# A bidirectional gated-delta scan: decay exponentials written into the decayed queries' tile, their loads issued earlier, and the last pair's norm work reordered

## What is computed

```python
def chunked_gated_delta(q, k, v, beta, log_alpha, s0):
    """S_t = a_t (I - b_t k_t k_t^T) S_{t-1} + b_t k_t v_t^T, o_t = S_t^T q_t"""
    g = jnp.cumsum(blk(log_alpha), axis=-1)
    a_mat = eye + einsum(kb, k) * dec_strict
    u_val = triangular_solve(a_mat, vb); w_key = triangular_solve(a_mat, kb * exp(g))
    qk = einsum(q, k) * dec_incl
    q_dec = q * jnp.exp(g)[..., None]
    k_end = k * jnp.exp(g_last - g)[..., None]
    def step(s, inp):
        v_new = u_c - w_c @ s
        o_c = qd_c @ s + qk_c @ v_new
        s = s * dl_c + ke_c^T @ v_new
        return s, o_c

def mixer(...):
    o_f, s_f = chunked_gated_delta(q, k, v, ...)          # forward
    o_b, s_b = chunked_gated_delta(rev(q), rev(k), ...)   # backward
    o = rmsnorm(o_f + rev(o_b), o_norm_w) * silu(gate)
    y = concatenate([y_conv, o]) @ w_out
```

## Time and profile before

| | us |
|---|---|
| median of 3 runs | 1591.64 |
| lowest, highest | 1590.41, 1592.5 |
| the profiled execution | 1592.61 |
| its span (first to last instruction) | 1590.7 |
| PE busy within it | 1524.4 (96%) |
| DVE, ACT, POOL busy | 936.8, 484.4, 403.1 |

### The profile page before, as it was taken

How to read it: one execution, slowest core, us unless ns; L and a number is a source line. 1 busy time by engine, 2 the same in 40 slices (tenths; PEclk the granted TensorE clock), 3 DMA queues, 4 the chain that set the end, 5 groups by cost and what they waited for, 6 DMA issues and landing times.

```text
span 1590.7 us, 24063 instructions
## 1 busy us (share of the span) xinstructions
PE 1524.4 (96%) x9744; PEld 1471.3 (92%) x9744; DVE 936.8 (59%) x1398; ACT 484.4 (30%) x904; POOL 403.1 (25%) x204
## 2 busy tenths in 40 slices
PE   5899999999989997999999999999999999999997
PEld 1798999999989887998999999999999999999996
DVE  2751463669987884337885276528643673467257
ACT  4332253221257675125311132121212210221024
POOL 0011111650233452130231123113222321223120
PEclk9999999999999998999999999999999999999999
DMA  9545124541434467120111111111111111111103
GB/s 360 217 158 184 68 82 127 158 128 70 141 114 127 142 205 268 40 67 1 40 54 41 41 40 43 51 41 40 40 40 41 47 47 40 41 40 40 40 1 119
DMA packets 74112, 142.60 MB, mean 90 GB/s; under 512 B 19212, under 2 KB 44372, under 8 KB 72340
## 3 DMA queue, kind: packets, MB, share of 16 engines
q1 hardware_dynamic: 70116, 131.38, 24.4%
q10 hardware_dynamic: 3456, 7.87, 1.3%
q0 software_dynamic: 432, 1.77, 0.3%
HBM read 120.34 MB, written 20.65 MB: 89 GB/s over the span
## 4 chain that ended last, share of the span: by engine, by line
PE 85%; DVE 7%; ACT 2%; issue 2%; DMA 2%; POOL 1%; DVEq 0%; ACTq 0%; SPq 0%; POOLq 0%
PE ps L2379 50%; PE ps L2381 25%; PE ps L1166 4%; DMA araw<-wts 2%; PE ps L2318 1%; DVE ptmp L1987 1%; DVE lanes L1991 1%; PE ps L2328 1%; POOL qd L698 1%; PE ps L2587 1%; DVE fa L2212 1%; DMA gb<-grow_d 1%; PE ps L2488 1%; PE ps L2447 0%; DVE XT L1998 0%
## 5 line engine op out<-in xcount | busy, mean ns | idle before, releaser
L2379 PE MATMUL ps<-hH,wH 128*128 128x384 f32 x1680 | 567.4, 338 | 7.7 <-DVE hL L1816 3.6
L2381 PE MATMUL ps<-hL,wH 128*128 128x384 f32 x1680 | 562.9, 335 | 0.0
L1292 POOL TENSOR_TENSOR wL<-raw,wH 128x1024 fp32r<-128x1024 f32 x93 | 226.1, 2431 | 886.0 <-ACT wH L1490 885.5
L2379 PE MATMUL ps<-hH,wL 128*128 128x384 f32 x1680 | 382.4, 335 | 0.0
L2379 PEld LDWEIGHTS ps<-hH,wH 128*128 128x128 f32 x1680 | 316.5, 188 | 15.6 <-issue 9.4
L1490 ACT ACTIVATE wH<-raw 128x1024 fp32r<-128x1024 f32 x99 | 105.1, 1062 | 716.8 <-PE ps L2379 715.0
L2381 PEld LDWEIGHTS ps<-hL,wH 128*128 128x128 f32 x1680 | 316.5, 188 | 0.0
L2212 DVE SCALAR_TENSOR_TENSOR fa<-G,cst,fa 128x1024 f32<-128x1024 f32 x176 | 295.9, 1681 | 15.4 <-DVE fa L2209 0.6
L2379 PEld LDWEIGHTS ps<-hH,wL 128*128 128x128 f32 x1680 | 300.3, 188 | 0.0
L2379 PE MATMUL ps<-pH,wH 128*128 128x384 f32 x528 | 179.3, 340 | 4.1 <-DVE pL L2236 1.9
L2099 DVE SCALAR_TENSOR_TENSOR X<-ps,mod,X 128x384 f32<-128x384 f32 x138 | 70.5, 566 | 188.8 <-PE ps L2379 188.8
(11 more groups left out here) (326 smaller groups left out, 1875.6 us busy)
## 6 DMA issues: line engine op xcount, KB each, us to landing
raw<-wts SPq DMA_DIRECT2D x103, 512.0 KB, 3.3
araw<-wts SPq DMA_DIRECT2D x48, 512.0 KB, 5.8
X<-xT SPq DMA_DIRECT2D x8, 1152.0 KB, 14.5
kv<-tok_d SPq DMA_DIRECT2D x16, 512.0 KB, 5.3
tok_d<-stage ACTq DMA_DIRECT2D x18, 256.0 KB, 2.0
gb<-grow_d SPq DMA_DIRECT2D x18, 256.0 KB, 3.8
q<-q_d SPq DMA_DIRECT2D x17, 256.0 KB, 6.1
y<-X SPq DMA_DIRECT2D x8, 384.0 KB, 2.4
```

The costliest lines, as they stand in the source:

```text
L1292: nc.gpsimd.tensor_tensor(weight(1, u4), raw[:, u4 % RAW, :], weight(0, u4).bitcast(F32), ALU.subtract).then_inc(s["wl_ready"], 1)
L2379: last = M(out, lhs, rh[:, c], start=(k == 0 and not lo), stop=(lo and k == kts - 1))
L2381: M(out, lhs, rl[:, c], start=False, stop=False)
```

## The change

Seven edits, none of which changes what is computed.

1. `gb_exps` writes into `qd` instead of in place; `decayed` multiplies `qd` by `q` in place. The exponential of step y waits until `qs` of the step before has read `qd`.
2. The load of `gb` (now `gb_load`) therefore waits for `gb_exp` and no longer for `q_decayed`. The first one (y = 1) is issued ahead of the first keys' and the last gate block's DMAs.
3. On PE `query_rows(0)` moves behind `with_state(1, 0)`.
4. On DVE, for y from 4 to 8, `values` stands behind the z copies, and so behind `new_state(1)`.
5. The last pair (i = 3) and the context tile (i = 4) get sums and roots of their own, in tiles `gB` and `gA`; they drop the waits for `o_ln` and `o_scaled`.
6. At x = 8 POOL squares the last pair before it scales the pair before; at the end it squares the context tile before it scales the last pair. ACT does the logarithms of both pairs together, then the roots of both.
7. At the end DVE sums the context tile's squares before it finishes a pair.

```diff
+            def gb_load(d, y):
+                seen(sp, "gb_exp", d, y)
+                r = tile_of(d, y) * 2 * H + d * H
+                sp.dma_start(dl[d]["gb"][:], grow_d[r:r + H, 1, :]...).then_inc(s[f"gb_in_{d}"], 16)
+
+            for d in range(2):
+                gb_load(d, 1)
             for d in range(2):
                 seen(sp, "vb", d, 1)
                 sp.dma_start(dl[d]["kv"][:, 0:H, :], ...)
...
-                    seen(sp, "q_decayed", d, y)
-                    sp.dma_start(b["gb"][:], ...)
+                if y > 1:
+                    for d in range(2):
+                        gb_load(d, y)
...
-            done(nc.gpsimd.tensor_tensor(qd_of(d, y)[:], gb_raw(d, y)[:], q_of(d, y)[:], ALU.mult), "q_decayed")
+            done(nc.gpsimd.tensor_tensor(qd_of(d, y)[:], qd_of(d, y)[:], q_of(d, y)[:], ALU.mult), "q_decayed")
...
-                    done(A(gb_raw(d, y)[:], gb_raw(d, y)[:], ACT.Exp), "gb_exp")
+                    if y:
+                        seen(nc.scalar, "qs", d, y)
+                    done(A(qd_of(d, y)[:], gb_raw(d, y)[:], ACT.Exp), "gb_exp")
...
-                    for d, t, i in summed(x - 1):
+                    for d, t, i in summed(x - 1) + summed(x):
                         log_mean(d, i)
-                    for d, t, i in summed(x - 1):
+                    for d, t, i in summed(x - 1) + summed(x):
                         root(d, i)
...
-                seen(dve, "o_ln", d, i)
+                if i < 3:
+                    seen(dve, "o_ln", d, i)
...
-                if pre:
+                if 0 < y < HALF:
                     for d in range(2):
-                        if y:
-                            values(d, y)
+                        values(d, y)
...
+                if HALF <= y < TT_:
+                    for d in range(2):
+                        values(d, y)
...
-                if x == 0:
-                    query_rows(0)
                 if x == 0:
                     pe.wait_ge(side_free[(N_Z - 1) % 2], (N_Z - 1) // 2 + 1)
                 if scan and x < LAST:
                     with_state(1, x)
+                if x == 0:
+                    query_rows(0)
```

More of the change, by code:

```diff
@@ L451, in gb_raw, with red_of, rs_of @@
         return dl[d]["gb" if y else "gb0"]
+    def red_of(d, i):
+        return dl[d]["red"][:] if i < 3 else gB[:, 2 * (i - 3) + d, 0:H]
+    def rs_of(d, i):
+        return dl[d]["rs"][:] if i < 3 else gA[:, 2 * (i - 3) + d, 0:H]
     def R_of(d, y):
@@ L627, in _ @@
                     q_load(0, y)
-                for d in range(2):
-                    b, t = dl[d], tile_of(d, y)
-                    seen(sp, "q_decayed", d, y)
-                    r = t * 2 * H + d * H
-                    sp.dma_start(b["gb"][:], grow_d[r:r + H, 1, :].unsqueeze(0).broadcast_to([P, H, P])
-                                 ).then_inc(s[f"gb_in_{d}"], 16)
+                if y > 1:
+                    for d in range(2):
+                        gb_load(d, y)
                 for d in range(2):
@@ L710, in scale @@
                 seen(pool, "o_rs", d, i + 1)
-                done(gp.tensor_tensor(oTok[:, t], oTok[:, t], along(b["rs"][:], P), ALU.mult), "o_scaled")
+                done(gp.tensor_tensor(oTok[:, t], oTok[:, t], along(rs_of(d, i), P), ALU.mult), "o_scaled")
             for x in range(TT_):
@@ L719, in delta_pool @@
                     low(U_OUT + 1, U_OUT + 1)
-                for d, t, i in summed(x - 1):
-                    scale(d, t, i)
+                if x < LAST:
+                    for d, t, i in summed(x - 1):
+                        scale(d, t, i)
                 for d, t, i in summed(x):
@@ L724, in delta_pool @@
                     square(d, t, i)
+                if x == LAST:
+                    for d, t, i in summed(x - 1):
+                        scale(d, t, i)
                 if y < TT_:
@@ L730, in delta_pool @@
                             decayed(pool, d, y)
+            seen(pool, "o_add", 0, TT_)
+            square(0, LAST, 4)
             for d, t, i in summed(LAST):
                 scale(d, t, i)
-            seen(pool, "o_add", 0, TT_)
-            square(0, LAST, 4)
             scale(0, LAST, 4)
@@ L852, in log_mean @@
                 seen(act, "o_sum", d, i + 1)
-                seen(act, "o_scaled", d, i)
-                done(A(b["rs"][:], b["red"][:], ACT.Ln, scale=1.0 / P, bias=biases[:, 1:2]), "o_ln")
+                if i < 3:
+                    seen(act, "o_scaled", d, i)
+                done(A(rs_of(d, i), red_of(d, i), ACT.Ln, scale=1.0 / P, bias=biases[:, 1:2]), "o_ln")
             def root(d, i):
@@ L858, in root @@
                 seen(act, "o_ln", d, i + 1)
-                done(A(b["rs"][:], b["rs"][:], ACT.Exp, scale=-0.5), "o_rs")
+                done(A(rs_of(d, i), rs_of(d, i), ACT.Exp, scale=-0.5), "o_rs")
             def key_end(d, y):
@@ L924, in delta_act @@
                     high(U_OUT + 1, U_OUT + 1, 0)
-                if x != LAST - 1:
+                if x < LAST - 1:
                     for d, t, i in summed(x):
@@ L1045, in delta_dve @@
                     diagonal(y)
-                if x == LAST:
-                    for d, t, i in summed(x):
-                        sum_squares(d, t, i)
                 if pre and y:
```

12 lines of the change are left out of this document (8 added, 4 removed).

## The result

| | before | changed |
|---|---|---|
| median of 5 runs, us | 1591.64 | 1580.73 |
| lowest, highest | 1590.04, 1596.84 | 1575.79, 1584.97 |
| the profiled execution | 1592.61 | 1575.79 |
| its span | 1590.7 | 1574.0 |

The ratio is 0.9928 (95% interval 0.99 to 0.9956): faster by 10.9 us. The forecast was 20.3 us, and 1580.73 lies 1.7 us above the range. Measured again beside 14 other runs of the kernel before, the changed kernel came to 1578.72 against 1594.43, ratio 0.9895 (0.9873 to 0.9917), 15.7 us. The two intervals overlap; all ten runs of it lie between 1575.8 and 1585.0. The forecast is missed by 5 to 9 us either way.

A forecast was written before the change was run, and what follows sets the result against it. PE, with 85% of the chain, bounds the kernel; only its idle or half-clock time can be won. Terms -4.3 -5.8 -0.6 -1.1 +1.3 -9.8 = -20.3 from 1592.61, less 1.0 to the median: 1571.3 us, range 1565 to 1579.

The forecast's parts named there:

- the three large stops: PE idle 4.08 us in step 0, 2.78 in step 4 and 7.01 behind step 8; all forecast to shrink or go.
- Step 5: Scan step after step 4; the prediction gave it no term of its own.
- step 7: Moved values delay the weights PE waits for: 0.62 us becomes about 1.9, +1.3 (0.5 to 1.5).
- step 6: PE's waits on POOL's scaling and the z copy shrink or go: -0.6 and -1.1 us.
- Step 0: Scan's start: earlier gb loads bring to_state from 478.04 to 474.7, less clock loss; -4.3 us (-1 to -7).
- Steps 1 to 3: Masks come earlier, but PE has no wait there: 0 us.
- step 4: Earlier gb loads end PE's wait before to_state and the half clock behind it: -5.8 us (-3 to -6).
- costs twice: Each large PE stop also brings half clock behind it; about 6 us at half speed loses 3 us of work.
- The end part: Behind step 8: projection starts without the 7.01 us stop, at full clock: -7.0 and -2.8, together -9.8 us (-7 to -11).
- the rivals: Step 0 gives nothing 0.15, end only part 0.07, step 4 stays 0.06, clock never falls in step 0 0.10, slower 0.02.
- the sum of all small ends: Every term at its least favourable end at once: -9.5 us, that is 1582.
- The slower rival: Port exclusion stretches POOL's pair by 3.7 us before PE in all seven steps: +26, 1597 us; chance 0.02.

The follow-up runs named there:

- experiment 5: Changed kernel with the last pair's part undone in order and waits (POOL scales before squaring, logarithms pair by pair, DVE finishes before summing): 1587.28 us, ratio 0.9966.
- experiment 6: Changed kernel with the exponential written in place and the gb load waiting for q_decayed again, for y from 2: 1584.38 us, ratio 0.9952.
- experiment 7: Changed kernel with the first gb loads behind the gate store again and query_rows(0) ahead of with_state(1, 0): 1584.47 us, ratio 0.9945.
- experiment 1: The changed kernel measured and profiled again, nothing edited: median 1578.72 us, ratio 0.9895.
- experiment 8: Changed kernel with the two halves of the keys loaded ahead of the first two gb loads: 1579.33 us, ratio 0.9901.
- experiment 3: The kernel before with only DVE's values moved behind the z copies for y of 4 to 8: 1597.39 us against 1590.92, ratio 1.0039.
- experiment 2: Changed kernel with DVE's values put back ahead of the z copies in all steps: 1575.05 us, ratio 0.988.
- experiment 10: Changed kernel with keys, gb and the first q loads ahead of the gate store, and values back ahead of the z copies: 1571.07 us, ratio 0.9861.
- experiment 4: A second profile of the kernel before and a third of the changed kernel, nothing edited: 1591.2 and 1580.69 us.

## Why the prediction was wrong by half, and where it was right

In short: the three large stops went as forecast. What failed is the account of edit 4. Step 5 was entered at 0 and came at +2.1 us, the half clock behind the longer wait of step 7 was entered at 0 and came in every profile, and the gain in step 6 was read off waits that a second execution does not show.

**The bound and the three large stops: right.** Only PE's idle time and its half clock could be won, and the three stops that I listed are all gone. Undoing each part brings its own stop back (experiments 5 to 7).

**Step 0: the mechanism right, the sum right in two of three executions, and partly by luck.** I said `to_state` at 474.7; it came at 476.51. One microsecond of that is a later start of the scan in that execution. The rest is the keys: I had them land near 468, 5.4 us after the time they were issued at before, and they landed at 469.94. From there on the working holds: 3.08 us from the keys to PE's release (3.06 forecast) and 3.5 us more to `to_state` (3.6). The stop was 2.80 us where I wrote "about 2", because of the keys. The half clock behind the stop, of which I took half of 3 us, was all or nothing here: none in two profiles, 1.7 us in the third. Forecast -4.3; -4.2, -2.5 and -4.3 came. That the sum was met is in part luck. In the first profile the start of `to_state` moved by 2.6 us against the scan's start (13.82 to 11.24) and not by 3.3; a wait of 0.92 us stood behind it where I had put 0.5; and the clock, entered at -1.5, gave about 2.6, since it didn't fall at all.

**Steps 1 to 3 and step 4: right.** 0 and -5.7, for 0 and -5.8. Undone, step 4 costs 5.0 us.

**Step 5: the step that failed.** The sum has no term for it. Of edit 4 I wrote that the z copies "now wait only for PE's own products", and I looked for the cost of the moved values in step 7 alone, where a wait on the weights stood in the rows. I did not walk down DVE's list behind them: in step 4 the same displacement falls on `second_out`, which frees the bank of PE's next `with_state`, and PE waited 1.35 us for it; step 5 took 15.84 us against 14.24, and 17.36 or 18.59 where the half clock followed (experiments 1 and 8).

Most of the 1.35 us is an overlap. In all seven profiles that have this wait, the values in step 4 took 2.53 to 2.55 us beside POOL's product, and PE's second group of step 5 began 2.5 us after its first. In the two with edit 4 and without edits 1 and 2 for this step (experiments 3 and 6), POOL's product was over before the values began; they took 1.28 us, the second group began 1.25 us after the first (1.0 before), and step 5 took 14.57. The differences are 1.26 and 1.27 us. So the order alone costs 0.3 us, and the rest is DVE beside POOL, which edit 4 together with the vanished stop in step 4 brought about. For step 4 the prediction had written "Next late is the solve itself"; next late, one step on, were DVE's additions. Without edit 4 the overlap can still fall on either side: in experiment 2 it drew out DVE's weights (2.34 us) and PE waited 0.64, in experiment 10 it drew out POOL's product (4.43 us), and PE did not wait.

**Step 6: read off one execution.** I took 1.00 and 0.61 us as the kernel's; a second execution shows 0.47 and nothing. Against it the whole gain of step 6 is 0.3 us. Most of what I took for a property of the order belonged to one execution.

**Step 7 and the solve behind it: the wait right, its clock left out.** 0.62 became 1.82, forecast 1.9. But each large stop "costs twice", as I had written of the others, and I did not ask that of this one. In all nine profiles with edit 4 the wait is 1.82 us and the solve behind it takes 3.40 to 3.75 us. In the four without it, it took 2.02 us three times and 3.63 once, in the one that I had read. The half clock at this place, 1.6 us, was there in one execution of the kernel before and not in the other; with edit 4 it is always there. The other part of the +2.3 of step 7 stands at its start, where PE waits 0.69 us for the output tile (0.3 before, by the starts of its first two groups): the values of step 6 took 1.86 us, again beside POOL's product. With edit 4 undone the piece from step 8 to the projection is 5.41 us, 8.0 less than the mean before; with it, 6.0 less.

**Edit 4 in all** was entered at +0.2 (-1.1 and +1.3). Undoing it gave -3.7 us by the medians and -4.7 us in the pieces from step 5 on; alone in the kernel before it cost 6.2. It is the largest single cause of the miss.

**The end part: right.** The projection's first matmul follows the last product, at full clock, and the turns found their tiles ready. Counted from that matmul, ACT's roots of both pairs were there after 0.8 us (604.5 - 603.7) where I had 2.5 (613 - 610.5), because the sums no longer wait, and POOL's last scaling ended after 7.6 us (611.3) where I had 6.5 (617); no wait of PE for it shows. -2.8 for -2.8, and the stop gone.

**The account of the miss.** The forecast for the scan was -20.3. Against the profile that I read it from, the mean of three profiles is -16.5 (154.9 - 171.4); the 3.8 missing are step 5 (2.1), step 7 (1.0) and step 0 (0.6); the rest nearly cancels. A second profile of the kernel before is 3.2 us shorter in the scan than that one, which takes 1.6 from the mean: -14.9. The timed runs gave -10.9 and -15.7, two draws of five runs each. What else differs between the profiles is the prologue: the scan's start lies anywhere from 464.2 to 471.1 us in the profiles of these kernels, which share that part, and the profile that I read had the earliest of them. The three of the changed kernel start it 2.4 us later than the two of before, on average, which takes as much from the gain. Most of the spread arises early, around a stretch where the clock is low. Two stretches of the changed kernel without edit 4 and with it, in the order of the earlier trace rows:

```profile
44.00:46.00 2.00, 1.46 (x4) 0.00 (x0) 1.36 (x2) 0.49 (x2) 0.00 (x0) 0.50 1.04 411
```

```profile
44.00:46.00 2.00, 0.32 (x3) 0.23 (x3) 0.17 (x1) 1.44 (x3) 0.00 (x0) 0.62 1.01 399
```

The first of these executions (scan start 471.06) is at the half clock from 37 to 56 us, the second (465.27) from 45 to 51. The code up to there is the same. By the matmuls done, the first is about 5 us behind the second at 60 us, of 5.8 at the scan's start. That this varies is shown, and over the runs of the changed kernel a lower mean clock goes with a longer time (1575.79 us at 0.990, 1584.97 at 0.985). What makes it vary in the prologue wasn't tried and stays open. It also means that my "1.0 above the median" made too much of one execution: its time was near the median by a short prologue and a long scan.

**The range and the rivals.** None of the rivals happened as written. The measured 1580.73 lies between the end of the range and 1582, the sum of all small ends, which I had worked out and left outside. The range also left out a term of the wrong sign in a step that I had put at 0, and the spread of the changed kernel itself, 6 to 9 us over five runs. The slower rival, at 0.02, asked for POOL's stretch ahead of PE in all seven steps, and that did not come. Its mechanism did, on DVE's side, in the values of step 4 (1.26 us more) and of step 6 (0.6 more), at places that it did not name.

## What to carry to other kernels

When a block is moved down an in-order engine's list, walk every instruction behind it down to the next step, not only the one that waits in the trace now, ask which instruction of another engine will run beside the block at its new place, and ask of each new wait of more than a microsecond what the clock costs behind it too. Read each small wait in at least two executions before it is entered as a gain: in two profiles of one kernel here the large stops repeated to 0.02 us, and of the small waits those of 0.62 and 0.68 did and those of 0.61 and 1.00 did not. When several loads are moved ahead of a large store, order them by who needs them first, and move the last of them too: moving gb alone made the keys late, moving the keys made q late, and all three together, with edit 4 undone, gave 1571.07.

## What the runs showed of the hardware

- The half clock behind a stop is not a fixed function of its length here. Stops of 4.1 us in step 0, 2.8 us in step 4 and 7.0 us behind step 8 had it in both profiles of before, one of 1.82 us in step 7 in all nine profiles with edit 4, and one of 2.44 us on the q load in the one profile of experiment 8. The 0.62 and 0.68 us in the place of the 1.82 had it in one of four. The stop on KQ in step 0 (2.66 to 2.80 us; experiments 1, 4, 5, 6 and the first profile) had it in one profile of five, and the wait of 1.35 us in step 5 in two of seven (17.36 and 18.59 us for the step, 15.84 in the others). What PE ran ahead of the stop differs between these places, and the runs don't separate that.
- How long a load takes depended on its place in the queue: the keys' halves were there 2.8 us after issue when they stood first, and 5.3 us behind two loads of gb. Experiment 8 changes nothing but this order, and has 2.8 again.
- Two multiplications of 128x512 by DVE took 1.28 us alone (step 7) and 2.54 us where POOL multiplied beside them (step 4), and POOL's own pair took 2.95, for 2.51 alone (experiment 6). Which side is drawn out differs: in experiment 10 DVE's pairs took 1.28 us and POOL's 4.43.
